# Ten single adaLN units in each feed-forward, a second weight buffer for two more in the first, an earlier load for group 1, and one wait less in the mixers

## The reference

```
cs = jax.nn.silu(c)
for l in range(DEPTH):
    mod = (cs @ ada_w[l] + ada_b[l]).reshape(B, N_SUB, 3, D_MODEL)[:, :, :, None, :]
    h = _rmsnorm(x, norm_g[l, 0]) * (1.0 + mod[:, 0, 1]) + mod[:, 0, 0]
    x = x + 0.5 * mod[:, 0, 2] * _swiglu(h, ffn_w_gate[l, 0], ffn_w_up[l, 0], ffn_w_down[l, 0])
    h = _rmsnorm(x, norm_g[l, 1]) * (1.0 + mod[:, 1, 1]) + mod[:, 1, 0]
    x = x + mod[:, 1, 2] * _mixer(h, w_in[l], conv_w[l], w_conv_out[l], w_attn_out[l], w_o[l], rel_bias)
    h = _rmsnorm(x, norm_g[l, 2]) * (1.0 + mod[:, 2, 1]) + mod[:, 2, 0]
    x = x + 0.5 * mod[:, 2, 2] * _swiglu(h, ffn_w_gate[l, 1], ffn_w_up[l, 1], ffn_w_down[l, 1])
```

## Time and profile before

| | |
|---|---|
| median of three runs | 2287.4 us |
| profiled execution, its own time | 2291.7 us |
| its span on the core | 2289.4 us |
| busy, PE / DVE / ACT | 2124.3 / 1437.5 / 1008.6 us |
| DMA, mean over the span | 191 GB/s |

### The profile page before, as it was taken

The page is one execution under the profiler, slowest core; times in us unless marked ns, Lnnn a source line. Parts: engine busy times, 40 slices in busy tenths (PEclk is TensorE's granted clock), DMA queues, the critical chain, the costliest instruction groups (busy, mean ns, idle before and its releaser), DMA issues.

```text
span 2289.4 us, 29825 instructions
## 1 busy us (share of the span) xinstructions
PE 2124.3 (93%) x12031; PEld 1850.6 (81%) x12031; DVE 1437.5 (63%) x1893; ACT 1008.6 (44%) x1249; POOL 31.4 (1%) x57
## 2 busy tenths in 40 slices
PE   6988899999989999889999999998999877799998
PEld 5767688999878878678989998886888766797887
DVE  5766577568676666567766776545544566656544
ACT  3433343444444353335434445435444456546433
POOL 0000000000000000000000000000000000000000
PEclk9989899999999999999999999999999888899999
DMA  8676579446668648666865575553655422255652
GB/s 273 226 234 216 171 241 297 120 143 221 202 230 259 223 152 271 206 209 207 278 190 144 169 251 195 186 184 122 229 184 184 129 88 88 93 186 172 203 186 90
DMA packets 355916, 438.09 MB, mean 191 GB/s; under 512 B 9563, under 2 KB 323355, under 8 KB 355780
## 3 DMA queue, kind: packets, MB, share of 16 engines
q1 hardware_dynamic: 350592, 420.51, 56.4%
q0 software_dynamic: 4160, 14.23, 2.8%
q10 hardware_dynamic: 1028, 1.45, 0.2%
HBM read 435.05 MB, written 1.11 MB: 191 GB/s over the span
## 4 chain that ended last, share of the span: by engine, by line
PE 67%; DVE 14%; DMA 7%; ACT 6%; issue 3%; DVEq 2%; SPq 1%; ACTq 0%
DMA raw<-in_ada_w 7%; PE PC L1470 5%; PE PA L1463 5%; PE PC L1472 5%; PE PC L1471 5%; DVE lo L951 5%; PE PA L1470 5%; PE PA L1472 4%; PE PA L1471 4%; PE PA L1464 4%; PE PA L1465 4%; DVE acc L964 4%; PE PB L1470 4%; PE PB L1472 4%; PE PB L1471 4%
## 5 line engine op out<-in xcount | busy, mean ns | idle before, releaser
L951 DVE TENSOR_TENSOR lo<-raw,hi 128x2048 fp32r<-128x2048 f32 x277 | 633.4, 2289 | 280.9 <-ACT hi L591 280.4
L591 ACT ACTIVATE hi<-raw 128x2048 fp32r<-128x2048 f32 x277 | 528.7, 1910 | 319.5 <-PE PC L1472 205.0
L1463 PE MATMUL PA<-nl,hi 128*128 128x256 f32 x976 | 291.2, 298 | 14.5 <-issue 9.7
L1464 PE MATMUL PA<-nh,lo 128*128 128x256 f32 x976 | 283.8, 291 | 0.0
L1465 PE MATMUL PA<-nh,hi 128*128 128x256 f32 x976 | 283.3, 290 | 0.0
L964 DVE SCALAR_TENSOR_TENSOR acc<-raw,cs,acc 128x256 f32<-128x256 f32 x483 | 234.1, 485 | 37.7 <-issue 1.8
L1470 PE MATMUL PA<-hi,nl 128*128 128x512 f32 (+1 forms) x528 | 211.8, 401 | 17.1 <-DVE nl L1025 17.1
L1463 PEld LDWEIGHTS PA<-nl,hi 128*128 128x128 f32 x976 | 195.7, 201 | 16.8 <-issue 10.5
L1470 PE MATMUL PC<-hi,cL 128*128 128x512 f32 x384 | 158.9, 414 | 53.1 <-DVE cL L1097 53.1
L1472 PE MATMUL PA<-hi,nh 128*128 128x512 f32 (+1 forms) x528 | 207.8, 394 | 0.0
L1471 PE MATMUL PA<-lo,nh 128*128 128x512 f32 (+1 forms) x528 | 207.5, 393 | 0.0
(11 more groups left out here) (276 smaller groups left out, 3876.7 us busy)
## 6 DMA issues: line engine op xcount, KB each, us to landing
raw<-in_w_in SPq DMA_DIRECT2D x90, 1024.0 KB, 5.9
raw<-in_ada_w SPq DMA_DIRECT2D x72, 1024.0 KB, 7.4
raw<-in_ffn_w_gate SPq DMA_DIRECT2D x88, 512.0 KB, 4.2
raw<-in_ffn_w_up SPq DMA_DIRECT2D x88, 512.0 KB, 5.3
raw<-in_ffn_w_down SPq DMA_DIRECT2D x44, 1024.0 KB, 5.0
raw<-in_ffn_w SPq DMA_DIRECT2D x88, 512.0 KB, 4.7
raw<-in_ffn_w SPq DMA_DIRECT2D x22, 1024.0 KB, 4.9
raw<-in_w_o SPq DMA_DIRECT2D x12, 1024.0 KB, 5.2
```

The lines of the kernel that those rows point to most:

```text
L591: A(parts_of(n)[0], raw[:, n % 3, :], ACT.Copy).then_inc(hi_done, 1)
L951: V.tensor_tensor(l, raw[:, n % 3, :], h.bitcast(F32), ALU.subtract).then_inc(lo_done, 1)
L1463: MM(o, wh[:, c0:c0 + w], xl, start=first, stop=False, skip_group_check=True)
L1464: MM(o, wl[:, c0:c0 + w], xh, start=False, stop=False, skip_group_check=True)
```

## The change

`ffn_ada` places one unit in each of the groups 1 to 10 of stages 0, 2 and 3, and two extra ones only in stage 0, in groups 4 and 7 (`TWICE`). Stage 2 thereby has 10 units, stage 3 has 10, stage 0 still 12. The two extra units get a buffer of their own, `ada_second`, in memory that was padding, with a semaphore of its own. Their loads stand after the second weights of group 4 and 7, in the loop iterations 2 and 5, so more than a group ahead of their use. The load of group 1's unit stands before the first weights of group 1. The unit of group 10 is loaded behind the stage's last weights. The wait `arrive(c + 2)` in the mixers of the first block goes.

```
-    phases = {0: (0, 8, 1, 8), 2: (3, 0, 3, 9), 3: (3, 9, 4, 8)}
+    phases = {0: (0, 8, 1, 8), 2: (3, 0, 3, 10), 3: (3, 10, 4, 8)}
...
-    twice = (4, 6, 8)[:len(units) - 9]
...
-    for i in range(1, NG - 1):
+    for i in range(1, NG):
         mid[i] = next(units)
-        end[i] = next(units) if i in twice else None
+        end[i] = next(units) if s == 0 and i in (4, 7) else None
...
+TWICE = [ada_no(*u) for u in ffn_ada(0)[1] if u]
+
+def ada_full(n):
+
+    return n + 3 - sum(k < n for k in TWICE)
...
-            sb("pad_a", [P, 2 * D], F32, r)
+            ada_b = sb("ada_second", [P, 2 * D], F32, r)
...
                 p, u = unit
                 n = ada_no(p, u)
...
+                if n in TWICE:
+                    if n == TWICE[0]:
+                        sp.wait_ge(lines_out, 32)
+                    else:
+                        sp.wait_ge(ada_used, TWICE[0] + 1)
+                    sp.dma_start(ada_b, src).then_inc(ada_full2, 16)
+                    return
+                if n == 0:
+                    sp.wait_ge(ada_d, 5)
                 else:
-                    sp.wait_ge(ada_d, 5)
...
+                    sp.wait_ge(ada_used, n - 1 if n - 1 in TWICE else n)
+                sp.dma_start(raw[:, 3, :].rearrange("p (k f) -> p k f", k=KC), src).then_inc(raw_full[3], 16)
...
                 up(0, 0)
                 up(0, 1)
+                load_ada(mid[1])
                 up(1, 0)
                 up(1, 1)
                 load(b + down_unit(0), d_v[0])
                 for i in range(NG - 2):
                     up(i + 2, 0)
-                    load_ada(end[i] or mid[i + 1])
+                    if i:
+                        load_ada(mid[i + 1])
                     up(i + 2, 1)
+                    load_ada(end[i + 2])
                     load(b + down_unit(i + 1), d_v[i + 1])
-                    if end[i]:
-                        load_ada(mid[i + 1])
                 load(b + down_unit(NG - 1), d_v[NG - 1])
+                load_ada(mid[NG - 1])
...
                     ada(end[i])
                     split(b + 3 * i + 4)
+                ada(mid[NG - 1])
                 split(b + 32)
...
                     c = b + 18 + 3 * j
-                    if j == 0:
-                        arrive(c + 2)
                     for u in range(3):
                         arrive(c + u)
```

More of the change, by code:

```diff
@@ L260, in build @@
             ub_b = sb("ub_b", [P, KC, P], F32, r)
+        ada_b = ada_b[:, :].rearrange("p (k f) -> p k f", k=KC)
         xc, gl, ra, ig, lt, lw = (acc[:, i * 512:(i + 1) * 512] for i in range(6))
@@ L309, in build @@
         raw_full = [sem(f"raw_full{i}") for i in range(4)]
+        ada_full2 = sem("ada_full2")
         ada_d, ada_p, ada_used = sem("ada_d"), sem("ada_p"), sem("ada_used")
@@ L421, in load_ada @@
                 n = ada_no(p, u)
[L422 to L428 removed]
+                src = ada_v[p // 3][:, :, (p % 3) * 3 * D + u * UC:(p % 3) * 3 * D + (u + 1) * UC]
+                if n in TWICE:
[7 more added lines that the diff above has]
+                    sp.wait_ge(ada_d, 5)
+                else:
+                    sp.wait_ge(ada_used, n - 1 if n - 1 in TWICE else n)
+                sp.dma_start(raw[:, 3, :].rearrange("p (k f) -> p k f", k=KC), src).then_inc(raw_full[3], 16)
             def ffn(s, g_v, u_v, d_v):
@@ L954, in after, with ada_unit @@
                 dve.wait_ge(unit_done, n + 1)
-            def ada_unit(col, slot, full, done):
-                dve.wait_ge(raw_full[slot], full)
-                w = raw[:, slot, :].rearrange("p (k f) -> p k f", k=KC)
+            def ada_unit(col, w, done):
                 o = acc[:, col:col + UC]
@@ L967, in ada @@
             def ada(unit):
-                if unit is not None:
-                    ada_unit(unit[1] * UC, 3, (ada_no(*unit) + 3) * 16, ada_used)
+                if unit is None:
+                    return
+                n = ada_no(*unit)
+                if n in TWICE:
+                    dve.wait_ge(ada_full2, (TWICE.index(n) + 1) * 16)
+                    ada_unit(unit[1] * UC, ada_b, ada_used)
+                else:
+                    dve.wait_ge(raw_full[3], ada_full(n) * 16)
+                    ada_unit(unit[1] * UC, raw[:, 3, :].rearrange("p (k f) -> p k f", k=KC), ada_used)
             def mods(p):
@@ L1232, in _ @@
                     normed(0, 0)
-                ada_unit(u * UC, u % 4, (u // 4 + 1) * 16, ada_d)
+                dve.wait_ge(raw_full[u % 4], (u // 4 + 1) * 16)
+                ada_unit(u * UC, raw[:, u % 4, :].rearrange("p (k f) -> p k f", k=KC), ada_d)
             split(0)
```

## The result

The changed kernel takes 2221.7 us (median of four executions, 2221.06 to 2226.43), against 2287.4 us before: a ratio of 0.9715 with a 95% interval of 0.9699 to 0.9732. That is 65.7 us less, of the 74.4 us forecast. The profiled execution took 2226.4 us (span 2224.1), 65.3 us less than the profiled one of before.

The account below looks back on a forecast made before the run. PE, busy 93% of the span, bounds the kernel and waits on DVE, held by late adaLN loads. Feed-forwards 68.15 plus mixers 6.3 give 74.4 us: 2291.7 to 2217.3 profiled, 2213 as median; range 2207 to 2224, 2208 to 2220 alone.

Parts of the forecast that it names:

- signs that the prediction gave for being wrong: adaLN loads over 10 us to land, `cL` waits in stage 0's groups 5 and 8, or a feed-forward's end longer.
- Group 1, the earlier load: Stages 0, 2, 3: loading group 1's unit earlier leaves PE waits of 1.8, 0.5 and 0.5 us; delayed weights cost nothing.
- The double groups: Stage 0, groups with two units: DVE's extra 4.21 us delays `low` at most 3.03 against 3.95 us slack; no PE wait.
- The first rival: Stage 0's double groups still make PE wait, two groups costing 11.3 us: 2224; chance 0.13.
- The ring of single units: Feed-forwards: load, unit and split take 14.8, at most 16.6 us, under PE's 16.90 per group; the tenth unit costs nothing.
- The third rival: adaLN loads served with those behind them land after 13.2 us, pacing every group: slower than before, 2313; chance 0.02.
- The mixers' wait: First-block mixers: dropping the wait wins 3.15 us twice, 6.3 us; a 3.3 us gap at DVE's maximum stays, at full clock.
- The term's lower value: Mixers: if the remaining gap halves PE's clock, a half costs 1.46 us more and 3.4 us are won for both.
- The second rival: Mixers win only 3.4 us or nothing, and the ring is late once a stage: 2221, or 2219; chance 0.14.
- The row taken as witness: Stage 0 before: behind 3.44 us of PE idle the first matmul took 0.47 us, so the mixers' gap was put at full clock.

Follow-up runs that it names:

- one-buffer kernel: The changed kernel with both units of stage 0's double groups 4 and 7 through the one old buffer, loaded in the old order; 2244.6 us, ratio 0.9799.
- with the unit moved: The changed kernel, with DVE making the tenth adaLN unit behind attention steps 0 and 1 in first-block mixers, not ahead of step 0; 2212.6 us, ratio 0.9653.

## Why the prediction was right or wrong

The time, 2221.7, lies in the stated range of 2207 to 2224, and the sign and the main cause were right. It lies outside the 2208 to 2220 that the forecast gave for itself alone: only the two rivals' numbers make the range wide enough. The likeliest value was 8.7 us too low. Between the profiled executions 9.1 us are missing: 5.4 in the mixers, 0.6 in the feed-forwards, and the 3.1 elsewhere. Two of the signs that the prediction gave for being wrong did come: two loads took over 10 us to land, and two feed-forwards' ends became longer. Both are taken up below.

**Group 1, the earlier load: right.** Waits of 1.8, 0.5 and 0.5 us were forecast, 1.87, 0.47 and 0.47 came. The load one MB ahead of the weights cost nothing that shows: the first transposes of stage 0 come at 70.76 us, against 71.09 before. Putting it back cost 11.2 us in stages 2 and 3 by the rows, and did nothing to the wait in stage 0, where DVE's small terms set the time, as the prediction had it.

**The double groups: right.** No wait followed groups 4 and 7. DVE's idle time took in the second unit, and the one-buffer kernel shows that without the buffer the two groups cost 21 us. The first rival (2224) is out as a mechanism, though its number came near.

**The ring of single units: right up to the tenth transposes.** Stages 2 and 3 took 154.1 us there, against 153.9 forecast. That the tenth unit costs nothing behind them is not shown; see the last part.

**The third rival: out.** It decided from landings of 12.1 us on. The loads of the ring kept 7.4 us in the median. The two of the second buffer landed after 11.7 us, close to that point, but they left more than a group ahead, and nobody waited for them. The formula of the Trainium skill ("DMA: Bandwidth & Descriptors", "Anatomy of one DMA") is fitted to transfers issued from GpSimd, while SP issues these loads; the estimate of 6.8 us made from it lies 0.6 us under the measured median.

**The mixers' wait: the step that failed.** The prediction found the new gap, its length (3.3 us) and its releaser. It then said: "The nearer row is the first, so I take the full clock." The gap did cost the clock: six profiled executions have it, in both mixers, at 3.3 us (3.66 in one place). With no gap, the scores of step 2 start 4.84 us after those of step 1 (364.73 to 369.57, with the unit moved); behind the gap it took 7.7 to 7.9 us ten times of twelve, some 3 us more, and 6.3 us twice, 1.5 us more. So 3.15 us won in a mixer became 0.06 and 0.9 us (by the kernel with the wait alone dropped) and the term of 6.3 became 0.9. The rule of the Trainium skill ("TensorE: Matmul & The Clock Gate", "Why this matters for your kernels"), that idle gaps of PE between bursts of matmuls halve its clock, was given as the one that would make the sum smaller; these twelve gaps agree with it, the gap of 3.44 us in stage 0 of before (clock 1.00 behind it) does not.

The term's lower value, 3.4 us for both, was still too high; the measured 0.9 lies between it and the "nothing" that the prediction named last. The 3.4 charged 1.46 us for the half clock, from one half product, where the slow stretch behind the gap covers scores, transposes and most of a half. The second rival had the mechanism (the mixers at 3.4 or nothing, from a gap that stays), and its time, 2219 to 2221, is nearer the measured one than the forecast's 2213. Its other half, a ring late once in each stage, did not happen.

The row taken as witness was also read too far. Its first matmul took 0.47 us, and its window is indeed at full clock, but one place is one sample. In the kernel with group 1's load put back, and in the one with the unit moved, the first matmul behind a gap took 0.47 us too, and the clock fell behind it all the same. These are the windows from the gap's end to the next transposes: before, behind a gap of 3.44 us in stage 0:

```profile
80.60:93.20 12.60, 12.56 (x57) 10.45 (x58) 8.88 (x13) 2.85 (x4) 0.00 (x0) 1.00 1.00 332
```

with the load put back, behind a gap of 3.91 us in stage 2:

```profile
622.40:635.00 12.60, 12.57 (x49) 10.24 (x49) 9.48 (x13) 2.12 (x2) 0.00 (x0) 0.86 1.00 334
```

and with the unit moved, behind a gap of only 1.86 us in stage 0:

```profile
79.95:92.60 12.65, 12.62 (x49) 10.21 (x50) 8.37 (x12) 2.30 (x2) 0.00 (x0) 0.87 0.98 330
```

The same gap of 1.85 to 1.88 us kept its clock in three other runs (in the changed kernel 11.0 us from the gap's end to the next transposes, against 12.6 here), and was followed by a fall in the kernel with group 1's load put back (0.86). Six gaps of 3.91 to 5.23 us in group 1 all had a fall behind them (clock 0.80 to 0.88), one of 2.89 us had none. So a single row at full clock doesn't say that a gap is free, and the length of a gap alone does not decide.

**The 3.1 us in other places: put at nothing in the prediction, and partly settled.** One load in the tail of stage 1 landed late and held DVE for 1.31 us, in the timeline of after; neither before nor the second run of the changed kernel has this wait (the kernel with group 1's load put back has it, 1.15 us):

```profile
507.35 0.35 DVE L976 TENSOR_SCALAR acc<-raw,cs 128x256 f32<-128x256 f32 x1 [1.31 <-DMA raw<-in_ada_w]
```

Two waits of PE for splits follow it, 0.67 us at 517.97, where the other two have none, and 1.07 us at 530.81, where they have 0.60: 1.1 us of the 1.4 in that part.

The other part is the clock where stages end, in or right behind the 32 small matmuls that sum the modulation over the partitions. The end of stage 3, before and after (the timeline up to the next stage's first product, then the window):

```profile
1043.21 3.63 PE L1511 MATMUL PB<-ones,acc 128*128 128x1 f32 x32
1046.70 1.07 PE L1528 MATMUL PC<-ident,xn_a 128*128 128x128 f32 x8
...
1055.77 1.09 PE L1528 MATMUL PC<-ident,xn_a 128*128 128x128 f32 x8 [1.16 <-DVE xn_a L1006]
...
1058.94 0.47 PE L1470 MATMUL PB<-hi,nl 128*128 128x512 f32 x1 [0.67 <-DVE nl L1025]
...
1043.00:1047.00 4.00, 4.00 (x37) 3.96 (x36) 3.38 (x5) 0.24 (x1) 0.00 (x0) 1.00 0.00 0
```

```profile
976.87 4.38 PE L1535 MATMUL PB<-ones,acc 128*128 128x1 f32 x32
981.11 1.95 PE L1552 MATMUL PC<-ident,xn_a 128*128 128x128 f32 x8
...
994.46 0.47 PE L1494 MATMUL PB<-hi,nl 128*128 128x512 f32 x1 [0.69 <-DVE nl L1047]
...
978.00:982.00 4.00, 4.00 (x28) 4.00 (x28) 2.61 (x4) 0.00 (x0) 0.00 (x0) 0.69 0.15 17
982.00:986.00 4.00, 4.00 (x13) 3.32 (x13) 2.80 (x8) 2.85 (x8) 0.00 (x0) 0.50 0.67 245
```

The same matmuls run at full clock in one and fall to half speed in the other. The two windows after hold some 6.5 us at half clock (0.31 x 2 of the first 4 us, and all of the next), which cost half of that, 3.2 us. Part of it is hidden, since PE of before waits 1.16 us for DVE here: from the tenth transposes to the next stage's first product it is 32.30 us (962.16 to 994.46), against 30.44 before (1028.50 to 1058.94), so 1.9 us are lost. In stage 2 it is 32.28 against 31.51, 0.8 us lost, and in stage 0 30.67 against 31.22, 0.55 us won.

This is the prediction's sign "if a feed-forward's end became longer by the tenth unit". The tenth unit is not what PE waits for: the trace has no such wait there, and in the kernel with the mixers' unit moved the same end of stage 2 takes 30.45 us, with the tenth unit and the clock at 1.00. What makes these ends long is the clock. Over the ten profiled executions they fall into two kinds, 30.4 to 31.6 us with no fall or a short one, and 32.3 us with a long one. Of the six ends with the old placing of the units (before, and the wait alone dropped) none is long; of the 24 with the new placing 13 are, among them those of stages 2 and 3 in both runs of the changed kernel. At the ends of the mixers, where the change moves nothing, one of four and four of 16 have such a long fall. So the change may make the long falls more frequent in the feed-forwards, at some 2 us in all for stages 0, 2 and 3. Whether it does, and by what, stays open: executions are few, and no run changes the tenth unit alone.

## What to carry to other kernels

When a wait is dropped, follow the same stretch to the point where the engine is in step again, and count there: a gap moved from the convolution to the scores, and with the slow clock behind it all but 1 us of 6.3 was gone. A DVE task with no deadline (the adaLN unit) belongs behind the task that TensorE waits for (the maximum of the scores); moving it was worth 6.3 to 6.4 us in each mixer. For a stream with one buffer, a second buffer for the two places where two transfers follow one another, with their loads put earlier, was worth 21 us, and a load put earlier by one group's weights 11 us, both with no instruction less.

## What the runs showed of the hardware

- A gap of PE of 3.3 us in the mixers (3.66 in one place) cost its full clock in twelve places of twelve, with 3 us lost in ten and 1.5 in two. In group 1 of the feed-forwards a gap of 1.85 to 1.88 us cost either nothing or 1.6 us, run by run (two of five); gaps of 2.89 and 3.44 us cost no clock, and six of 3.91 to 5.23 us all did (a clock of 0.80 to 0.88 up to the next transposes).
- The first matmul behind a gap (0.47 us or 0.76 us) is no measure of the clock behind it; the granted clock of the whole stretch is.
- PE lost its clock at stage ends without being idle, in or right behind 32 one-column matmuls (0.79 and 1.00 over the same 8 us in two runs of the same kernel). How much a fall costs depends on the waits behind it: that one made the stage 0.25 us longer, the fall at the end of stage 3 1.9 us.
- A 1 MB adaLN load landed after 7.4 us in the median, but after 11.7 us where SP had issued three other MB in the 4.2 us before it (the second buffer's loads, the first issued at 97.34 behind loads from 93.12 on).
